# Two narrow projections as columns of wider groups, gate weights on two strips of rows, and other due tiles for VectorE

## Chip, cores and metric

One core of a Trainium2 chip runs one transformer stack of two different blocks for a batch of one with 256 tokens and a model width of 1024, in float32. The metric is the device time of one launch in microseconds (us), as the median of several runs.

## What is computed

The first block has attention over compressed, selected and window keys, retention, gates and an MLP. The change touches mainly the second block's mixer, in which one projection of the normed rows is split into ten parts:

```python
proj = n @ w_in
z, xBC, dt_raw, q, k, v, r, a1, g_ssd, g_gla = jnp.split(proj, idx, axis=-1)
# widths: z 1024, xBC 1536, dt_raw 16, q 512, k 512, v 1024, r 1024, a1 16, g_ssd 1024, g_gla 1024
# ssd: xBC = silu(causal conv of xBC);  dt = softplus(dt_raw + dt_bias);  a = -dt * exp(A_log)
#      y = (chunked scan of xs, B, C with steps dt and decays a) * silu(z), then a norm
# gla: log_alpha = log_sigmoid(a1 @ w_a2 + b_a) / 16;  w_a2 is 16 x 512
#      o = gated linear attention of q, k, v with these decays, normed, * silu(r)
merged = sigmoid(g_ssd) * (y_ssd @ w_up_ssd) + sigmoid(g_gla) * (y_gla @ w_up_gla)
```

In the kernel "the steps" are dt_raw (columns 2560 to 2575 of the weights) and "the gate's columns" are a1 (5648 to 5663).

## The kernel before

**Weights.** All 309 weight tiles go through one pipe, in one order. `weight` (L333) makes a tile of at most 1024 columns of float32 per partition. SyncE loads tile i into one of RAW = 4 raw buffers once VectorE has done tile i - 4 (L2318 is its issue). ScalarE rounds it to a high part (`round_tile`, L1014, instruction L1020), VectorE subtracts to get the low part (`rest_of_tile`, L1520, instruction L1524); both parts lie in one of PARTS = 5 buffers, which tile i gets when TensorE has released tile i - 5. A product is three matmuls: high by high, high by low, low by high.

**Groups.** `fm` (L353, matmuls L367 to L369) gives outputs with features on partitions: a group is 256 columns of weights, two tiles, 48 matmuls of 256 columns of tokens; the first tile is released after 36 of them, the second with the last. `tm` (L378, matmuls L398 to L400) gives outputs with tokens on partitions: a group of up to 512 columns of weights in two PSUM banks (one per half of the tokens), eight rows of blocks in four tiles, 12 matmuls a tile. `narrow` (L411) takes both sets of 16 columns as two tiles of 128 columns and 24 matmuls (L424 to L426).

**Order on TensorE.** `fill` (L792) is a chain of groups: z, gq, gk, gv, r, sig2, then a projection up. `step(n)` (L431) takes n steps from it, a step being a tile of tm or half a group of fm. The conv groups cv 2 to 5 are taken between by `conv()` (L788); cv 0 and 1 come ahead in `lead` (L479 to L481). From L796 on: a step, cv 2, two transposes that spread the rows' scales (L463), `narrow`, two steps, two transposes of the steps to tokens (L804), cv 3, two steps, cv 4, two steps, cv 5, two steps, then xs, the decays, and the loop over eight diagonal blocks (`diags`) with a step or two between and y's blocks turned by `y_out`. Behind it comes `la`, the product of wa2 (16 rows on partitions 0 to 15) with a1T, eight steps, the scores ST and ST2 of the gated attention (L350 is `group`, the helper of all small products) and its outputs.

**Order on ScalarE and VectorE.** Each goes through a list of operations written out in program order. Between them stand weight tiles: `until(v)` (L1023, L1527) first does all tiles whose parts buffer is released before TensorE's count v, and the drains "put behind" that are due before v, the earlier first and drains first at a tie; `full(name)` does `until` of that group's end and then waits for it. TensorE counts one for a released tile and one for an ended group.

```python
def until(v):
    while True:
        tile_at = gives_back(hi) if hi < len(tiles) else NEVER
        if min(tile_at, behind_at) >= v:
            return
        if behind_at <= tile_at:
            behind_at = next(behind, NEVER)
        else:
            round_tile()
```

ScalarE's list after the spread (L1314 on): conv copies of cv 0 and 1 (`conv_in`, L1306, two instructions each), two scaled copies of x (L1322), conv copies of cv 2, Exp of A_log (L1325), exponential of the steps (L1328), conv copies of cv 3, two silus (L1300), cv 4, and so on. Put behind: the drains of z with Silu (L1165), gv, r. VectorE's list: the spread copy (L1617), drains of conv groups into `craw` (L1558, a helper of all its two-operand instructions), for each group a conv of six L1564 (which waits for ScalarE's conv copies), the a1T drain (L1893), bias and minimum of the steps (L1898), a memset and the rest of the softplus. POOL computes a polynomial of it. Later VectorE adds up y's blocks, scales them (L1561), makes the operands ke and qe of the gated attention (L2067 on), and copies ST2 (L2078).

**In the first block** VectorE does `scores(1)`, `weigh(0)` and then for each p `weigh(p + 1)`, `scores(p + 2)`, with the due tiles only inside `scores` (L1779 on); ScalarE has an `until` of its own ahead of each exponential (L1227). L639 is the first matmul of the products with the values, which needs a copy of ScalarE (L1054).

## Time and profile before

| | us |
|---|---|
| three runs | 974.34, 974.57, 972.91 |
| median | 974.34 |
| the profiled execution | 972.9 |
| its span, first to last instruction | 971.1 |

The profile is one execution. A row of a timeline has the start in us from the span's start, the duration in us, the engine, the line, the operation, what it writes and reads, its shape and count, and in brackets idle time of the engine ahead of it with what ended that. PE is TensorE (PEld its weight loads), DVE VectorE, ACT ScalarE. Ends of matmuls are modelled and overlap, so the pace of matmuls is read from their starts. The granted clock of TensorE was 0.999 of full speed over the span.

### The profile page before, as it was taken

What the parts mean: (1) busy time and instruction counts of PE and PEld (TensorE: products, weight loads), DVE (VectorE), ACT (ScalarE), POOL (GpSimd) and SP (SyncE); (2) the same over time, 40 slices, a digit from 0 to 9 for tenths busy, and PEclk for the clock granted to TensorE, in tenths of its full rate; (3) what the DMA queues carried; (4) which work ended last, traced back from release to release, by engine and by line L of the source; (5) the groups of instructions that cost most, each with busy time, mean ns of one, the idle gap of its engine ahead of it and who ended that gap; (6) DMA issues with size and microseconds to landing.
All of it is one profiled execution on the core that took longest, in us unless ns stands there. A gap on an engine that the chain in (4) does not pass through costs nothing.

```text
span 971.1 us, 15946 instructions
## 1 busy us (share of the span) xinstructions
PE 959.3 (99%) x6548; PEld 869.1 (89%) x6548; DVE 626.0 (64%) x811; ACT 516.7 (53%) x785; POOL 59.8 (6%) x110
## 2 busy tenths in 40 slices
PE   9999999999999999999999999999999999999997
PEld 7877789989998888999988999998998899999996
DVE  5776775677555555778857787776554466555544
ACT  6576645656444544566865565644455445444443
POOL 3000001001000000304000002100000010000001
PEclk9999999999999999999999999999999999999999
DMA  9972635455665656466564455555655446565661
GB/s 307 311 237 65 181 108 163 164 174 176 212 191 181 188 181 189 124 196 190 155 194 132 129 173 187 159 184 172 200 164 157 125 153 215 177 198 172 194 194 44
DMA packets 135528, 170.37 MB, mean 175 GB/s; under 512 B 7856, under 2 KB 99296, under 8 KB 135456
## 3 DMA queue, kind: packets, MB, share of 16 engines
q1 hardware_dynamic: 133488, 165.20, 55.2%
q10 hardware_dynamic: 1424, 2.84, 0.8%
q0 software_dynamic: 544, 1.31, 0.4%
q8 instruction: 52, 0.85, 0.3%
q14 instruction: 20, 0.16, 0.1%
HBM read 168.28 MB, written 1.05 MB: 174 GB/s over the span
## 4 chain that ended last, share of the span: by engine, by line
PE 88%; DVE 5%; ACT 3%; issue 2%; POOL 0%; DMA 0%; ACTq 0%; POOLq 0%; DVEq 0%
PE ps L367 13%; PE ps L369 13%; PE ps L368 13%; PE ps L398 8%; PE ps L400 7%; PE ps L399 7%; PE ps L725 5%; PE ps L724 5%; PE ps L723 5%; PE ps L350 4%; PE ps L448 3%; DVE parts L1524 2%; DVE room L1558 2%; PE ps L479 1%; PE ps L481 1%
## 5 line engine op out<-in xcount | busy, mean ns | idle before, releaser
L1524 DVE TENSOR_TENSOR parts<-raws,parts 128x1024 fp32r<-128x1024 f32 (+2 forms) x309 | 367.8, 1207 | 233.0 <-ACT parts L1020 232.2
L1020 ACT ACTIVATE parts<-raws 128x1024 fp32r<-128x1024 f32 (+2 forms) x309 | 316.1, 1040 | 242.6 <-PE ps L369 136.2
L367 PE MATMUL ps<-room_r,parts 128*128 128x256 f32 x1248 | 352.2, 282 | 0.1
L368 PE MATMUL ps<-room_r,parts 128*128 128x256 f32 x1248 | 348.5, 279 | 0.0
L369 PE MATMUL ps<-room_r,parts 128*128 128x256 f32 x1248 | 348.4, 279 | 0.0
L367 PEld LDWEIGHTS ps<-room_r,parts 128*128 128x128 f32 x1248 | 234.6, 188 | 5.7 <-issue 3.9
L368 PEld LDWEIGHTS ps<-room_r,parts 128*128 128x128 f32 x1248 | 234.7, 188 | 1.3
L369 PEld LDWEIGHTS ps<-room_r,parts 128*128 128x128 f32 x1248 | 234.6, 188 | 0.0
L398 PE MATMUL ps<-parts,room_r 128*128 128x512 f32 (+1 forms) x336 | 134.8, 401 | 1.4 <-DVE parts L1524 1.4
L400 PE MATMUL ps<-parts,room_r 128*128 128x512 f32 (+1 forms) x336 | 131.1, 390 | 0.0
L399 PE MATMUL ps<-parts,room_r 128*128 128x512 f32 (+1 forms) x336 | 131.0, 390 | 0.0
L723 PE MATMUL ps<-parts,room_r 128*128 128x512 f32 x204 | 80.7, 396 | 0.0
L725 PE MATMUL ps<-parts,room_r 128*128 128x512 f32 x204 | 80.7, 396 | 0.0
L724 PE MATMUL ps<-parts,room_r 128*128 128x512 f32 x204 | 80.7, 396 | 0.0
L398 PEld LDWEIGHTS ps<-parts,room_r 128*128 128x128 f32 x336 | 63.2, 188 | 16.3 <-DVE parts L1524 2.4
L400 PEld LDWEIGHTS ps<-parts,room_r 128*128 128x128 f32 x336 | 63.1, 188 | 14.4
L399 PEld LDWEIGHTS ps<-parts,room_r 128*128 128x128 f32 x336 | 63.2, 188 | 13.2 <-issue 0.5
L1558 DVE TENSOR_TENSOR room_r<-room,room_r 128x512 fp32r<-128x512 f32 x43 | 29.8, 693 | 33.1 <-ACT room_r L1285 11.9
L725 PEld LDWEIGHTS ps<-parts,room_r 128*128 128x128 f32 x204 | 38.3, 188 | 9.3
L723 PEld LDWEIGHTS ps<-parts,room_r 128*128 128x128 f32 x204 | 38.3, 188 | 8.2
L724 PEld LDWEIGHTS ps<-parts,room_r 128*128 128x128 f32 x204 | 38.3, 188 | 8.1
L350 PE MATMUL ps<-room 128*128 128x256 f32 (+6 forms) x276 | 43.1, 311 | 0.7 <-DVE room L2078 0.7
(225 smaller groups left out, 877.5 us busy)
## 6 DMA issues: line engine op xcount, KB each, us to landing
raws<-in_w_in SPq DMA_DIRECT2D x99, 512.0 KB, 4.5
raws<-in_w_ffn_in SPq DMA_DIRECT2D x44, 512.0 KB, 4.4
raws<-in_w_up SPq DMA_DIRECT2D x32, 512.0 KB, 4.1
raws<-in_w_down SPq DMA_DIRECT2D x32, 512.0 KB, 4.1
raws<-in_w_ffn_out SPq DMA_DIRECT2D x22, 512.0 KB, 4.2
raws<-in_w_xkv SPq DMA_DIRECT2D x16, 512.0 KB, 4.1
raws<-in_w_out SPq DMA_DIRECT2D x8, 512.0 KB, 4.0
raws<-in_w_up_ssd SPq DMA_DIRECT2D x8, 512.0 KB, 4.5
```

The costliest lines, as they stand in the source:

```text
L350: last = e.matmul(ps, l, r, start=i == 0, stop=i == len(pairs) - 1)
L367: e.matmul(ps, wh, hT[0][:, k, :], start=k == 0, stop=False)
L368: e.matmul(ps, wh, hT[1][:, k, :], start=False, stop=False)
L369: last = e.matmul(ps, wl, hT[0][:, k, :], start=False, stop=k == K - 1)
L398: e.matmul(ps, hT[0][:, k, tok], wh, start=k == 0, stop=False)
L399: e.matmul(ps, hT[0][:, k, tok], wl, start=False, stop=False)
L400: last = e.matmul(ps, hT[1][:, k, tok], wh, start=False, stop=k == K - 1)
L723: e.matmul(ps, uh[:, k, tok], wh, start=q == 0 and k == 0, stop=False)
L724: e.matmul(ps, uh[:, k, tok], wl, start=False, stop=False)
L725: last = e.matmul(ps, ul[:, k, tok], wh, start=False, stop=q == n - 1 and k == 1)
L1020: e.activation(t.h, t.raw, ACT.Copy).then_inc(s["hi"], 1)
L1524: e.tensor_tensor(t.l, t.raw, t.h.bitcast(F32), ALU.subtract).then_inc(s["lo"], 1)
```

## The change

- The 16 columns of the steps become the last columns of z's first group, those of the gate the last of r's first group. z and r are now three groups each (THIRDS: 336, 352, 336 columns of their own, so 352, 352 and 336 with the added ones): 12 tiles and 144 matmuls each instead of 8 and 96. A tile of a first group is loaded by two DMAs.
- `narrow`, its two transposes and both its drains go.
- ScalarE drains the added columns: the steps straight into `dt3` (tokens on partitions already), the gate's columns of both halves of the tokens into `twice`. TensorE turns the latter to `a1T` in the loop at i = 7, VectorE copies that at i = 6 of its own list.
- The steps of `fill` are dealt out anew: 2, 2, 3, 3, 3 around the conv groups; two a round from i = 5 on; 4 after the loop.
- wa2 lies on two strips of rows (0 to 15 and 32 to 47), loaded by two DMAs; `la` goes strip by strip in turn.
- VectorE does due tiles after `weigh(0)`, with the bound that ScalarE has there, and ahead of ke and qe with ScalarE's bound instead of ST's end.

```diff
 
+        THIRDS = [(0, 336), (336, 352), (688, 336)]
...
+                elif also is not None:
+                    srcs = [(raw[:, :, 0:n - 16], src.rearrange("(k p) n -> p k n", p=P)),
+                            (raw[:, :, n - 16:n], also.rearrange("(k p) n -> p k n", p=P))]
...
-                for b0 in range(512 * first, cn, 512):
-                    nb = min(512, cn - b0)
+                spans = spans or [(b0, min(512, cn - b0)) for b0 in range(512 * first, cn, 512)]
+                for blk, (b0, n) in enumerate(spans, first):
+                    more = blk == 0 and also is not None
+                    nb = n + 16 if more else n
                     own = [bank(), bank()]
-                    tile_at = lambda k0, deep: weight(w[k0 * P:(k0 + deep) * P, c0 + b0:c0 + b0 + nb], deep, nb)
+
+                    def tile_at(k0, deep):
+                        rows_ = slice(k0 * P, (k0 + deep) * P)
+                        return weight(w[rows_, c0 + b0:c0 + b0 + n], deep, nb, also=w[rows_, also:also + 16] if more else None)
...
-            def narrow(name, parts_of, hT, ready):
...
-            fill = chain(tm("z", w2, 0, 1024, xT, x_ready(MIX2)), fm("gq", w2, 2576, 512, xT, x_ready(MIX2)),
+            fill = chain(tm("z", w2, 0, 1024, xT, x_ready(MIX2), spans=THIRDS, also=2560), fm("gq", w2, 2576, 512, xT, x_ready(MIX2)),
                          fm("gk", w2, 3088, 512, xT, x_ready(MIX2)), tm("gv", w2, 3600, 1024, xT, x_ready(MIX2)),
-                         tm("r", w2, 4624, 1024, xT, x_ready(MIX2)), fm("sig2", w2, 5664, 2048, xT, x_ready(MIX2)),
+                         tm("r", w2, 4624, 1024, xT, x_ready(MIX2), spans=THIRDS, also=5648), fm("sig2", w2, 5664, 2048, xT, x_ready(MIX2)),
                          fm(("first", 1), a["w_up_ssd_2"][0], 0, D, yT, lambda k: need(s["yT"], 4)))
-            step()
+            step(2)
             conv()
             spread_rstd(4, MIX2)
-            narrow("a1dt", [(w2, 5648), (w2, 2560)], xT, x_ready(MIX2))
-            step(2)
-            b = bank()
-            out_of("a1dt")
-            for t in range(2):
-                last = e.transpose(psum[:, b, 16 * t:16 * t + 16], a1T[32:48, t * P:t * P + P], ident[32:48, 32:48])
-            ends(last, "dt", b)
-            conv()
             step(2)
             conv()
-            step(2)
+            step(3)
             conv()
-            step(2)
+            step(3)
+            conv()
+            step(3)
...
-                step()
+                step(2 if i > 4 else 1)
                 if i == 7:
                     y_out(0, 1)
+                    need(s["a1"], 2)
+                    turn("a1T", [twice[:, half_, 0:48] for half_ in range(2)])
                 diag(t, q)
                 if i < 6:
                     step()
                 if i in (2, 4):
                     y_out(i // 2 - 1, 0)
-            step(3)
+            step(4)
             y_out(1, 1)
             step()
-            need(s["wa2"], 16)
-            for i in range(2):
-                b = bank()
-                for c in range(2):
-                    h = 2 * i + c
-                    last = group(psum[:, b, 256 * c:256 * c + 256], [(wa2[:, h * P:h * P + P], a1T[0:16, :])])
-                ends(last, ("la", i), b)
+            need(s["wa2"], 32)
+            out_of("a1T")
+            own = [bank() for _ in range(2)]
+            for c in range(2):
+                for i in range(2):
+                    h, strip = 2 * i + c, slice(32 * i, 32 * i + 16)
+                    last = group(psum[:, own[i], 256 * c:256 * c + 256], [(wa2[strip, h * P:h * P + P], a1T[strip, :])])
+                    if c:
+                        ends(last, ("la", i), own[i])
...
+            def thirds_out(dst, name, f, more, more_to):
+
+                for blk, (c0, n) in enumerate(THIRDS):
+                    for t in range(2):
+                        g = where[name, blk, t]
+                        yield g.at
+                        e.wait_ge(s["pe"], g.at)
+                        if blk == 0:
+                            to = more_to(t)
+                            e.activation(to, bc(psum[:, g.bank, n:n + 16], 1, list(to.shape)), ACT.Copy,
+                                         scale=scaled(MIX2, t)).then_inc(s[more], 1)
+                        e.activation(dst[:, t, c0:c0 + n], psum[:, g.bank, 0:n], f, scale=scaled(MIX2, t)).then_inc(taken[g.bank], 1)
+
             def projections2():
-                yield from tm_out(zs, "z", 2, MIX2, ACT.Silu)
+                yield from thirds_out(zs, "z", ACT.Silu, "dt", lambda t: dt3[:, t, :].unsqueeze(1))
                 yield from tm_out(gv, "gv", 2, MIX2)
-                yield from tm_out(gr, "r", 2, MIX2)
+                yield from thirds_out(gr, "r", ACT.Copy, "a1", lambda t: chunks(twice[:, t, 0:64], 2)[:, :, 0:16])
...
-            until(where["a1dt"].at + 1)
+            until(where["spread", MIX2].at + 2)
...
-            full("dt")
+            until(where["z", 0, 1].at + 1)
...
-            until(max(where["r", 1, 1].at + 1, where["la", 1].at + 6))
-            out_of(("r", 1, 1))
+            until(max(where["r", 2, 1].at + 1, where["la", 1].at + 6))
...
             scores(1)
             weigh(0)
+            until(where["S", 1, 1].at + 3)
...
-            full("a1dt")
-            emptied(tt(a1T[0:48, :], bank_of("a1dt")[0:48, 0:256], rows_rstd[0:48, :], ALU.mult), "a1dt")
             conv(0)
             conv_in(2)
-            until(where["a1dt"].at + 1)
+            until(where["spread", MIX2].at + 2)
             conv(1)
-            full("dt")
-            emptied(tt(dt3, bank_of("dt")[:, 0:32].rearrange("p (t h) -> p t h", t=2),
-                       bc(row("ssd_dt_bias_2"), 1, [P, 2, 16]), ALU.add), "dt")
-            out_of("dt")
+            until(where["z", 0, 1].at + 1)
+            e.wait_ge(s["dt"], 2)
+            step(tt(dt3, dt3, bc(row("ssd_dt_bias_2"), 1, [P, 2, 16]), ALU.add))
+            settle()
             stt(e_, dt_, -1.0, dt_, ALU.mult, ALU.min).then_inc(s["soft_e"], 1)
...
-                out_of(("z", 0, t))
-                out_of(("z", 1, t))
+                for blk in range(3):
+                    out_of(("z", blk, t))
...
+                if i == 6:
+                    full("a1T")
+                    emptied(e.tensor_copy(a1T[0:48, :], bank_of("a1T")[0:48, 0:256]), "a1T")
...
-            until(where["ST", 0].at)
+            until(max(where["r", 2, 1].at + 1, where["la", 1].at + 6))
...
```

The rest of the diff names the semaphore "a1", makes wa2 48 rows high and loads its two halves on POOL's queue.

## Rows read from the trace of the kernel before

**Rows 1.** The page's first part: each engine's busy us, and granted clock by slice

```profile
PE 959.3 (99%) x6548; PEld 869.1 (89%) x6548; DVE 626.0 (64%) x811; ACT 516.7 (53%) x785; POOL 59.8 (6%) x110
...
PEclk9999999999999999999999999999999999999999
```

**Rows 2.** Waits of TensorE: waited for, us in total, times, longest us

```profile
PE ps L639 <- ACT room L1054: 2.2, 1, 2.2
...
PE ps L398 <- DVE parts L1524: 1.4, 2, 0.8
...
PE ps L350 <- DVE room L2078: 0.7, 1, 0.7
```

**Rows 3.** Timelines of VectorE, ScalarE and TensorE, 92 to 100 us

```profile
92.22 0.18 DVE L1809 RECIPROCAL room<-room 128x4 f32<-128x4 f32 x1 [3.74 <-ACT big L1227]
...
93.25 4.62 DVE L1524 TENSOR_TENSOR parts<-raws,parts 128x1024 fp32r<-128x1024 f32 x4
...
98.14 1.06 ACT L1020 ACTIVATE parts<-raws 128x1024 fp32r<-128x1024 f32 x1 [5.07 <-DMA raws<-in_w_in]
...
99.73 0.49 PE L639 MATMUL ps<-room 120*128 120x128 f32 x2 [2.15 <-ACT room L1054]
```

**Rows 4.** Timeline of TensorE, 410 to 428 us, around the narrow product

```profile
410.63 0.39 PE L398 MATMUL ps<-parts,room_r 128*128 128x512 f32 x1
...
413.43 0.28 PE L367 MATMUL ps<-room_r,parts 128*128 128x256 f32 x1
...
419.17 0.36 PE L424 MATMUL ps<-room_r,parts 128*48 128x256 f32 x1
...
422.04 0.40 PE L398 MATMUL ps<-parts,room_r 128*128 128x512 f32 x1
...
427.74 0.29 PE L804 MATMUL ps<-ident,room 16*128 16x16 f32 x2
```

**Rows 5.** Timeline of ScalarE, 422 to 443 us

```profile
422.79 2.08 ACT L1306 ACTIVATE room<-room,cols 128x256 f32<-128x256 f32 x4 [2.44 <-DVE room L1558]
...
426.67 2.18 ACT L1322 ACTIVATE x<-room,ssq 128x1024 f32<-128x1024 f32 x2
...
429.85 1.28 ACT L1325 ACT_TABLE_LOAD   x1
...
441.30 1.28 ACT L1165 ACT_TABLE_LOAD   x1
...
442.60 1.26 ACT L1165 ACTIVATE room<-ps,ssq 128x512 f32<-128x512 f32 x2
```

**Rows 6.** Timeline of VectorE, 438 to 444 us

```profile
438.46 0.69 DVE L1558 TENSOR_TENSOR room<-ps,rows_rstd 128x512 f32<-128x512 f32 x1
...
443.05 1.22 DVE L1524 TENSOR_TENSOR parts<-raws,parts 128x1024 fp32r<-128x1024 f32 x1
```

**Rows 7.** Groups by line and shape: us busy, mean ns, idle before

```profile
L1020 ACT ACTIVATE parts<-raws 128x1024 fp32r<-128x1024 f32 x301 | 311.5, 1052 | 236.1 <-PE ps L369 136.2 <-PE ps L400 33.6 <-PE ps L725 33.4
...
L1524 DVE TENSOR_TENSOR parts<-raws,parts 128x1024 fp32r<-128x1024 f32 x301 | 363.1, 1223 | 232.0 <-ACT parts L1020 231.3
```

**Rows 8.** Timeline of TensorE: the gate product, and the first block's scores

```profile
545.70 1.99 PE L350 MATMUL ps<-room,wa 16*128 16x256 f32 x8
...
85.06 0.70 PE L613 MATMUL ps<-room 64*128 64x256 f32 x4
```

**Rows 9.** Timeline of VectorE, 572 to 577 us

```profile
572.87 2.36 DVE L1524 TENSOR_TENSOR parts<-raws,parts 128x1024 fp32r<-128x1024 f32 x2 [4.24 <-ACT parts L1020]
...
576.88 0.42 DVE L1558 TENSOR_TENSOR room<-room 128x256 f32<-128x256 f32 x1
```

**Rows 10.** Timelines of VectorE and TensorE around y's fourth turn

```profile
540.91 0.49 DVE L1561 TENSOR_SCALAR room<-room,ssq 128x512 f32<-128x512 f32 x1 [1.78 <-POOL ssq L2186]
...
542.36 0.60 PE L448 MATMUL ps<-ident,room 128*128 128x128 f32 x4
```

32 lines of the change are left out of this document (10 added, 22 removed).

## The prediction

> **What bounds the kernel now.** The page's first part is read first: TensorE is busy for 959.3 of 971.1 us, and its granted clock is at 9 tenths or more in all 40 slices [rows 1]. So TensorE's own columns set the time, and an edit counts where it takes instructions from that queue or makes it stand still. The waits of TensorE are read second: over 0.5 us there are few [rows 2]. L639 stands 2.2 us for a copy of ScalarE, L398 0.8 us (the longer of two) for VectorE's rest of a weight tile, L350 0.7 us for VectorE's last copy before the outputs of the gated attention. Third, the timelines of the other two engines around these places. Each works through a list in the program's order, and a weight tile needs both: ScalarE rounds it, VectorE takes the rest, and only then do its raw buffer (one of four) and, after its matmuls, its parts buffer (one of five) come free. What one engine does ahead of a tile is harmless only while TensorE has tiles in hand.
>
> **Part 1, due tiles before the first softmax (gain).** VectorE stands idle 3.74 us until 92.22, then weighs and takes four tiles in a row from 93.25 to 97.87, three of which ScalarE had rounded before its scores. ScalarE's next tile then waits 5.07 us for its DMA (98.14), whose raw buffer had been held by the first of the four, and TensorE's pv product stands until 99.73 behind it [rows 3]. The new `until` lets VectorE take the three in the idle time: 88.5 to 91.9, done before 92.22. The raw buffer is free at 89.6 instead of 94.4, and as release to rounding was 98.14 - 94.4 = 3.7 us, ScalarE has the tile at 93.3 and the copy by 94.9. TensorE starts its next tile without the 0.8 of L398 [rows 2], at 93.7, ends it at 96.5 and finds the copy there: 99.73 - 96.55 = 3.2, I take 3.1 us. Late next is nothing: VectorE's scores and ScalarE's exponentials move up by as much. Ends: 2.2 (the longer wait alone) and 3.3.
>
> **Part 2, columns.** Twelve matmuls of 512 columns take 410.63 to 413.43, so 0.2333 us each, 0.456 ns a column; the 48 of 256 behind them and two small transposes take until 419.17, 0.117 us each [rows 4]: time goes by columns, and nothing is charged per instruction at either width. So 352 columns are 0.160 us, 336 are 0.153. z was 96 x 512 columns, now 48 x 1040: 768 more, +0.35 us; r the same, +0.35. The narrow product goes: 419.17 to 422.04, -2.87 us, and its two transposes with the gaps around them, -0.4 [rows 4]. The new a1T turn adds two transposes of 0.11 each, +0.25 with its gap. Sum -2.3. Should 352 columns be charged like 512, z and r would cost 144 x 0.2333 instead of 96 x 0.2333, +11 each; the row of 256 excludes that.
>
> **Part 3, z's first group now holds the steps' columns (loss).** This is the large term, and I walk it in the clock of before; all of it hangs on order. TensorE, without waits: z0 and z1 (1.92 each) 410.63 to 414.5, conv group 2 (5.6) to 420.1, transposes to 420.2, z2 and z3 to 424.1, conv group 3 to 429.7, z4 and z5 to 433.55. Then it wants z6, whose parts buffer was z3's (free at 424.1).
> ScalarE [rows 5]: its four conv copies began at 422.79; one more tile ahead of VectorE's spread copy makes that 423.15. Copies 2.05, z5's tile 0.8, the two of L1322 2.1, conv copies 1.1, Exp's table load with its operation 1.4: 430.5. Now comes `until(where["z", 0, 1].at + 1)`, and the drains of z's first group are due before z6's tile: two copies of the steps 0.25, a load of Silu's table 1.28, two drains 1.05, so z6 is rounded from 433.0 to 433.8. Before, both drains came at 442.60, with the load of 441.30, after the exponential of the steps; now they stand between two Exp, so the exponential (L1328) and the first silu each need a load again: two more loads, 2.6 us. VectorE's rest: until 434.7. **Wait 1: 1.2 us.**
> VectorE adds the bias and makes its minimum (0.3), ScalarE waits for that, loads Exp (1.28), exponentiates (0.15) and only then rounds the next conv tile, 436.5 to 437.55; rest until 438.8. TensorE has wanted it since 434.8 + 1.92: **wait 2: 2.1 us.**
> VectorE drains group 3, from then on as before: from drain over ScalarE's copies and the conv to the tile behind it 443.05 - 438.46 = 4.6 us [rows 6]. The second tile of conv group 4 sits in the buffer of group 3's second tile, whose release is that group's very end, so both engines take it only after their conv work (before, it came a place sooner): 438.75 + 4.6 + 1.2 = 444.55 against a want at 438.9 + 1.4: **wait 3: 4.3 us.**
> The same pattern in group 5 leaves 0.5: its first tile's raw buffer is free at 444.55, landing and rounding take some 5.1, so its rest ends at 450.9; drain, conv and the tile behind (4.3 without the small work of group 3, and 1.2) give 456.4. TensorE ends group 4 at 448.8 and z7 to z9 at 454.5, and wants it at 455.9. **Wait 4: 0.5 us.** Sum +8.1 us. Tiles of 704 columns are taken as 0.80 on ScalarE and 0.89 on VectorE, from 1052 and 1223 ns for 1024 [rows 7]; 0.1 us either way moves each wait by as much. Bounds: 0 if the other order of drain and tile held, and 10.7 if either added load cost twice its row. The POOL queue gets one small DMA more and SP's queue eight pieces with 64-byte rows; they sit in transfers that land some us before their tile's turn.
>
> **Part 4, second gate weights.** Eight instructions on one strip take 545.70 to 547.62 [rows 8]. The scores of the first block use two strips: four take 0.70 us, the two first starting together. On strips the product of the gates should take about 1.05, -0.85 us; 0 if sixteen rows don't run side by side.
>
> **Part 5, later due tiles.** VectorE waits 4.24 us for ScalarE until 572.87 and makes the four decayed operands at 576.88, 1.1 us, after the tiles [rows 9]. With the smaller bound they go into the idle time, and the ST2 copy behind L350's wait [rows 2], which starts at 582.02, ends at 581.6 instead of 582.7. TensorE, earlier by part 4, then wants it at 582.0: the stall of 0.9 (the wait and its start) goes. Next late are tiles with about 1 us in hand.
>
> **Part 6, r and the turn.** From the turn of y's third block to that of the fourth TensorE has 9.3 us of work instead of 10.15 (four tiles of 336 columns for three of 512), and VectorE's chain there had y scaled at 541.4 against a turn at 542.36 [rows 10], with 0.4 added by the copy of a1T: +0.4 us. Ends 0 and 2.
>
> **Sum.** -3.1 - 2.3 + 8.1 - 0.85 - 0.9 + 0.4 = +1.35 us, taken as +1.4. The profiled execution was 972.9 us (span 971.1), hence 974.3; the median of the three runs is 974.34, 1.4 above it, so the forecast for a median is 975.7. About 0.2% (1.9 us) is what a measurement of this kernel can tell from no change, so this is no change.
>
> **A page that speaks against it.** After the load at 441.30 + 1.28 = 442.58 the drain starts at 442.60 [rows 5]: the load costs its own length. The Trainium skill's ScalarE: Activation LUTs, under What ACT_TABLE_LOAD costs, charges every switch of sets with 1283 ns and a drain of about 1380 more. By that rule the two new loads would cost 5.3 us instead of 2.6 and the result would be 978.4. As a mechanism of this kernel: an idle stretch of 1.4 us behind either load, passed on to waits 1 and 2. The rows speak against it, chance 0.02.
>
> **Rivals.** A, the forecast (0.55): own range 972.5 to 979. B, faster (0.23): ScalarE's delay is eaten by tiles in hand, or the conv tiles come in time; then the sum is 1.4 - 8.1 = -6.7, 967.6. For it: at present TensorE has no wait at all in this stretch, and the tiles in hand cover several us. Against: cover is five tiles, and z's have shrunk from 2.8 to 1.92 us each. C, slower (0.10): r's tiles are too short as well. Between conv and gate TensorE has 1.9 us per tile instead of 2.8 while ScalarE waits 3 to 4 us at a time on y's squares; once an engine is away from tiles for over 4 x 1.92 us plus the products between, TensorE stops. Two such stops of 1.5 us give +3: 978.7. D (0.05): part 1 does not do what it says, because the DMA and not VectorE's order was the limit; +3.1: 978.8. Against: that DMA began only after VectorE's release. E (0.05): TensorE's clock, at its upper level (2.4 GHz) in all slices now, even across the stand before 99.73, falls to the lower (1.2) during wait 3, twice as long; at half speed each us of matmuls costs another, and some 3 us of that give 978.7. The Trainium skill's TensorE: Matmul & The Clock Gate, under The HAM clock gate, has an idle array clocked down; no row here shows it in mid-kernel.
> Faster by over 0.2%: B and 0.06 of A, 0.29. Slower: C, D, E, the page's rule and 0.18 of A, 0.40. Within: 0.31. The range of 967 to 980 takes in B's centre, the slower rivals and the bounds of A.
>
> **What would show it.** Right: TensorE's waits at 94 to 100 gone, z and r at 0.16 us a matmul, four loads of tables between 425 and 450, and VectorE's rest of a tile as releaser of waits of some 1, 2 and 4 us between 430 and 445. Wrong: no wait over 1 us there (B), waits in the tiles of r (C), L639 still waiting (D), or 352 columns at over 0.17 us.

## The result: slower by half a per cent, and the profile after

The changed kernel took 978.59 us (median of 977.9, 979.1, 979.22 and 978.08) against 974.04 for the kernel before beside it: ratio 1.0048, 95% interval 1.0031 to 1.0065. So it is slower, by 4.5 us, where the forecast was 975.7 and no change; the range of 967 to 980 holds it. The profiled execution took 977.9 us with a span of 976.1, 5.0 more than before.

The page's first part and TensorE's granted clock by slice, as in [rows 1]:

```profile
PE 958.8 (98%) x6620; PEld 876.2 (90%) x6620; DVE 626.5 (64%) x817; ACT 522.1 (53%) x801; POOL 58.0 (6%) x111
...
PEclk9999999999999999999999999999999999999999
```

TensorE is as busy as before though it has fewer columns to go through. The waits of TensorE, to hold against [rows 2] (waited for, us in total, times, longest):

```profile
PE ps L373 <- DVE parts L1529: 6.7, 4, 4.0
PE ps L412 <- DVE parts L1529: 2.1, 2, 1.1
...
PE ps L442 <- DVE room L1566: 0.4, 1, 0.4
```

L639's wait (now L633) is gone, and VectorE's rest of a tile stands behind nearly all that is new: 8.8 us, of which 1.1 lies at the very start of the kernel (at 7.70; the kernel before waits 0.6 there). Where the rest is, the timeline of TensorE shows. A stand, a stretch in which TensorE starts nothing, is read here from start to start, less one matmul's own pace (437.14 to 441.40 is 4.26, less 0.12: 4.15 us); the idle time in brackets is 0.15 less, since it counts from a modelled end.

```profile
96.76 0.39 PE L633 MATMUL ps<-room 120*128 120x128 f32 x2
...
407.56 0.32 PE L412 MATMUL ps<-parts,room_r 128*128 128x352 f32 x1
407.72 0.33 PE L413 MATMUL ps<-parts,room_r 128*128 128x352 f32 x1
...
431.84 0.43 PE L412 MATMUL ps<-parts,room_r 128*128 128x352 f32 x1 [1.01 <-DVE parts L1529]
...
435.78 0.36 PE L373 MATMUL ps<-room_r,parts 128*128 128x256 f32 x1 [1.72 <-DVE parts L1529]
...
437.14 0.28 PE L375 MATMUL ps<-room_r,parts 128*128 128x256 f32 x1
441.40 0.58 PE L373 MATMUL ps<-room_r,parts 128*128 128x256 f32 x1 [3.99 <-DVE parts L1529]
...
442.00 0.41 PE L375 MATMUL ps<-room_r,parts 128*128 128x256 f32 x1
...
444.55 0.28 PE L375 MATMUL ps<-room_r,parts 128*128 128x256 f32 x1
...
546.86 0.66 PE L442 MATMUL ps<-ident,room 128*128 128x128 f32 x4 [0.43 <-DVE room L1566]
...
550.25 1.13 PE L356 MATMUL ps<-room,wa 16*128 16x256 f32 x8
...
571.79 0.36 PE L373 MATMUL ps<-room_r,parts 128*128 128x256 f32 x1 [0.43 <-DVE parts L1529]
...
573.97 0.39 PE L373 MATMUL ps<-room_r,parts 128*128 128x256 f32 x1 [0.54 <-DVE parts L1529]
```

The first product with the values starts 3.0 us sooner than in [rows 3]. A matmul of 352 columns takes 0.16 us. Then come the stands: 1.2 us before 431.84, 1.9 before 435.78, 4.15 before 441.40, 0.6 at y's fourth turn (546.86), 0.6 and 0.7 before two tiles of the gates (571.79, 573.97). And behind the longest one matmuls of 256 columns follow each other at 0.213 us (442.00 to 444.55 are twelve of them) instead of 0.117. The windows say why (length, busy us of PE, PEld, DVE, ACT and POOL, granted clock, DMA share, GB/s):

```profile
442.00:444.00 2.00, 2.00 (x11) 2.00 (x11) 1.90 (x7) 0.82 (x2) 0.05 (x1) 0.50 0.68 187
...
446.00:450.00 4.00, 4.00 (x30) 4.00 (x30) 1.87 (x2) 2.00 (x3) 3.23 (x10) 1.00 0.57 172
```

For 3.4 us, from about 441 on, TensorE ran at its lower clock level (1.2 GHz). The page's slices of 24 us each still print a 9: a fall this short is seen only in windows.

ScalarE in the same stretch, to hold against [rows 5]:

```profile
427.48 0.26 ACT L1310 ACTIVATE room<-ps,ssq 128x16 f32<-128x16 f32 x1
427.75 1.28 ACT L1312 ACT_TABLE_LOAD   x1
429.05 0.54 ACT L1312 ACTIVATE room<-ps,ssq 128x336 f32<-128x336 f32 x1
...
430.88 1.28 ACT L1333 ACT_TABLE_LOAD   x1
432.18 0.23 ACT L1333 ACTIVATE room<-room 128x32 f32<-128x32 f32 x1
432.31 1.04 ACT L1012 ACTIVATE parts<-raws 128x1024 fp32r<-128x1024 f32 x1
...
437.33 2.37 ACT L1012 ACTIVATE parts<-raws 128x1024 fp32r<-128x1024 f32 x3
```

Two loads (427.75, 430.88) stand between the copies of the steps and the exponential, as the forecast had it, and the next operation starts 1.30 us after the start of each. And VectorE, against [rows 6] and, for the last two rows, [rows 10] and [rows 9]:

```profile
432.04 2.46 DVE L1569 SCALAR_TENSOR_TENSOR room<-room,cols 128x256 f32<-128x256 f32 x6
434.41 1.22 DVE L1529 TENSOR_TENSOR parts<-raws,parts 128x1024 fp32r<-128x1024 f32 x1
...
437.45 2.46 DVE L1569 SCALAR_TENSOR_TENSOR room<-room,cols 128x256 f32<-128x256 f32 x6 [1.22 <-ACT room L1298]
...
440.14 2.78 DVE L1529 TENSOR_TENSOR parts<-raws,parts 128x1024 fp32r<-128x1024 f32 x3
...
546.72 4.62 DVE L1529 TENSOR_TENSOR parts<-raws,parts 128x1024 fp32r<-128x1024 f32 x4
...
570.43 1.21 DVE L1529 TENSOR_TENSOR parts<-raws,parts 128x1024 fp32r<-128x1024 f32 x1
```

The tile that ends wait 3 is the first of the three at 440.14. ScalarE had rounded it by 438.3; VectorE took it only after the convolution of group 3 (437.45). The tile that ends wait 2 was rounded at 432.31, done by 433.4, and taken by VectorE at 434.41, after the convolution of group 2 (432.04).

The four tiles at 546.72 stand between VectorE's scaling of y and the next operation of y's chain. In the kernel before they are three, behind the scaling at 540.91 [rows 10]:

```profile
541.31 2.35 DVE L1524 TENSOR_TENSOR parts<-raws,parts 128x1024 fp32r<-128x1024 f32 x2
544.23 1.23 DVE L1524 TENSOR_TENSOR parts<-raws,parts 128x1024 fp32r<-128x1024 f32 x1 [0.57 <-ACT parts L1020]
```

### The profile page after: what moved, and what is told of

Its sections match the earlier page's. It is cut to its first block, busy times and chain, and to the rows that moved or that the text cites. A ratio compares the mean times of both kernels' runs of the same rounds, so it can differ in the third digit from the quotient of the medians.

```text
span 976.1 us, 16142 instructions
## 1 busy us (share of the span) xinstructions
PE 958.8 (98%) x6620; PEld 876.2 (90%) x6620; DVE 626.5 (64%) x817; ACT 522.1 (53%) x801; POOL 58.0 (6%) x111
## 4 chain that ended last, share of the span: by engine, by line
PE 91%; DVE 4%; ACT 2%; issue 1%; DMA 1%; SPq 0%; POOL 0%; POOLq 0%; DVEq 0%; ACTq 0%
PE ps L373 14%; PE ps L374 14%; PE ps L375 14%; PE ps L412 7%; PE ps L413 7%; PE ps L414 7%; PE ps L718 5%; PE ps L719 5%; PE ps L717 5%; PE ps L356 5%; PE ps L442 3%; DVE parts L1529 1%; PE ps L473 1%; PE ps L475 1%; PE ps L474 1%; DVE room L1563 1%
## 5 line engine op out<-in xcount | busy, mean ns | idle before, releaser
L1529 DVE TENSOR_TENSOR parts<-raws,parts 128x1024 fp32r<-128x1024 f32 (+4 forms) x315 | 368.4, 1187 | 239.1 <-ACT parts L1012 237.8
L1012 ACT ACTIVATE parts<-raws 128x1024 fp32r<-128x1024 f32 (+4 forms) x315 | 317.1, 1024 | 243.7 <-PE ps L375 137.9
L412 PE MATMUL ps<-parts,room_r 128*128 128x512 f32 (+3 forms) x368 | 140.7, 382 | 2.4 <-DVE parts L1529 2.1
L414 PE MATMUL ps<-parts,room_r 128*128 128x512 f32 (+3 forms) x368 | 136.6, 371 | 0.0
L413 PE MATMUL ps<-parts,room_r 128*128 128x512 f32 (+3 forms) x368 | 136.5, 371 | 0.0
L412 PEld LDWEIGHTS ps<-parts,room_r 128*128 128x128 f32 x368 | 69.2, 188 | 15.4 <-DVE parts L1529 3.6
L414 PEld LDWEIGHTS ps<-parts,room_r 128*128 128x128 f32 x368 | 69.1, 188 | 11.5
L413 PEld LDWEIGHTS ps<-parts,room_r 128*128 128x128 f32 x368 | 69.2, 188 | 10.7 <-issue 0.5
L719 PEld LDWEIGHTS ps<-parts,room_r 128*128 128x128 f32 x204 | 38.3, 188 | 9.3
L718 PEld LDWEIGHTS ps<-parts,room_r 128*128 128x128 f32 x204 | 38.3, 188 | 8.2
L717 PEld LDWEIGHTS ps<-parts,room_r 128*128 128x128 f32 x204 | 38.3, 188 | 8.2
```

The source lines that it names most:

```text
L412: e.matmul(ps, hT[0][:, k, tok], wh, start=k == 0, stop=False)
L413: e.matmul(ps, hT[0][:, k, tok], wl, start=False, stop=False)
L414: last = e.matmul(ps, hT[1][:, k, tok], wh, start=False, stop=k == K - 1)
L717: e.matmul(ps, uh[:, k, tok], wh, start=q == 0 and k == 0, stop=False)
L718: e.matmul(ps, uh[:, k, tok], wl, start=False, stop=False)
L719: last = e.matmul(ps, ul[:, k, tok], wh, start=False, stop=q == n - 1 and k == 1)
```

## Experiments

Each time is a median and stands beside runs of the kernel before on the same chip. The chips are not the same throughout, so it is the ratio to the kernel before that is compared from one experiment to another; the changed kernel's is 1.0048. "Less than the change" is the difference of the ratios in us. Rows are from one profiled execution of each kernel.

### The two bounds alone

The kernel before, with

```diff
             weigh(0)
+            until(where["S", 1, 1].at + 3)
...
-            until(where["ST", 0].at)
+            until(max(where["r", 1, 1].at + 1, where["la", 1].at + 6))
```

> The kernel before with the change's two VectorE bounds and nothing else. My theory: the first (three due tiles before the first softmax) gives 3.1 to 3.2 us at the first product with the values, the second (due tiles ahead of the four decayed operands) some 0.9 us at the ST2 copy; together about -4, 970 against a before of 974. Rival (the DMA of the tile was the limit, and the 3.2 us came from elsewhere in the change): no difference at the first product, about 973 to 974. Rival on the second bound: with the gate product on one strip nothing is gained there, -3.1.

Measured: 968.74 us against 973.84, ratio 0.9944 (0.9932 to 0.9956), the fastest kernel of this study. VectorE:

```profile
88.50 3.49 DVE L1524 TENSOR_TENSOR parts<-raws,parts 128x1024 fp32r<-128x1024 f32 x3
92.33 0.18 DVE L1809 RECIPROCAL room<-room 128x4 f32<-128x4 f32 x1 [0.34 <-ACT big L1227]
...
577.73 0.68 DVE L2079 COPY room<-ps 128x512 f32<-128x512 f32 x1
```

The three tiles now lie in what was idle time, and the reciprocal waits 0.34 us instead of 3.74 [rows 3]. TensorE's first product with the values starts at 96.61, 3.12 us sooner, and later landmarks 3.22 sooner, until the last bound adds its 0.9 at the outputs: the copy of ST2 ends at 578.41, and TensorE starts the outputs without a stand at 578.83. The span is 4.4 us shorter; the medians differ by 5.1, of which 0.7 is the spread between executions. Parts 1 and 5 are as predicted, each to 0.1 us, and the rival on the DMA is out. So all that belongs to the columns and to the strips costs 9.4 us of span (976.1 - 966.7).

### Silu drains of z later

```diff
-                yield from thirds_out(zs, "z", ACT.Silu, "dt", lambda t: dt3[:, t, :].unsqueeze(1))
+                for t in range(2):
+                    g = where["z", 0, t]
+                    yield g.at
+                    e.wait_ge(s["pe"], g.at)
+                    e.activation(dt3[:, t, :], psum[:, g.bank, 336:352], ACT.Copy, scale=scaled(MIX2, t)).then_inc(s["dt"], 1)
+                for blk, (c0, n) in enumerate(THIRDS):
+                    for t in range(2):
+                        g = where["z", blk, t]
+                        yield max(g.at, where["cv", 3].at + 1)
...
```

> The changed kernel, with ScalarE's six Silu drains of z held back until the first tile of conv group 3 is released; only the two copies of the steps are made when z's first group ends. No load of a table stands between the spread and the softplus any more. Theory (each of the three waits is set by what the two engines do ahead of one certain tile): wait 1 (1.17 us at z's seventh tile) goes, wait 2 (1.9) shrinks to about 1.2, wait 3 (4.15, at the second tile of conv group 4) stays, and so does the stretch at the lower clock: -1.7 us, about 976.9 against 978.6. Rival (the table loads and drains are the root of all three waits): all go, -7 or more, about 971.

Measured: 975.7 us, ratio 1.0019 (1.001 to 1.0028), 2.8 us less than the change. Stands: wait 1 gone, wait 2 at 0.9, wait 3 still 4.15, and again 3.4 us at the lower clock behind it. So the added loads and drains make wait 1 and half of wait 2, and nothing of wait 3. The rival is out. By the trace it gained 2.35 us in this stretch where I had 1.7: wait 2 shrank by 1.0 and not 0.7, and my two terms, 1.2 and 0.7, already made 1.9.

### The tile ahead of the convolution of group 3

```diff
# ScalarE
+            until(where["cv", 3].at + 1)
             conv_in(3)
# VectorE
             conv_in(3)
+            until(where["cv", 3].at + 1)
             conv(3)
```

> The changed kernel, with one more bound on ScalarE (ahead of its copies of conv group 3) and one on VectorE (ahead of the convolution of group 3): the tile whose buffer comes free with the first half of conv group 3 is done before that convolution and not after it. Theory: wait 3 falls from 4.15 us to 0.3 to 1, TensorE's clock does not fall behind it (3.4 us at the lower level, worth about 1.5), waits 1 and 2 stay: -4.5 to -5.3, 973.3 to 974.1. Rival (the tile is late by its landing or by what both engines did before, not by the place of the convolution): within 1 us of 978.6. Rival (the clock falls for the sum of the three waits, not for the third): 3.4 to 4 us gained and the stretch at the lower clock still there.

Measured: 973.68 us, ratio 0.9997 (0.9988 to 1.0006), 5.0 less than the change: one tile moved past one convolution takes back the whole loss, within the intervals. VectorE, and TensorE behind it:

```profile
436.96 1.21 DVE L1530 TENSOR_TENSOR parts<-raws,parts 128x1024 fp32r<-128x1024 f32 x1
438.27 2.46 DVE L1570 SCALAR_TENSOR_TENSOR room<-room,cols 128x256 f32<-128x256 f32 x6
```

```profile
450.99 0.39 PE L373 MATMUL ps<-room_r,parts 128*128 128x256 f32 x1 [1.26 <-DVE parts L1530]
```

This execution is 0.8 us behind the changed kernel's at wait 1 already (432.66 to 431.84); so the tile, done at 438.17, is ready some 4 us sooner than there (441.3). The clock stays at its upper level, waits 1 and 2 are as they were (1.2 and 1.9). From z's first matmul to the turn of xs the trace has 3.9 us less, the medians more; 4 to 5 us is what can be said. The price shows at 450.99: 1.4 us at the second tile of conv group 5, which is the forecast's wait 4. In the changed kernel it was hidden, since wait 3 and the slow matmuls gave the two engines over 5 us there.

### z without its silu

```diff
-                yield from thirds_out(zs, "z", ACT.Silu, "dt", lambda t: dt3[:, t, :].unsqueeze(1))
+                yield from thirds_out(zs, "z", ACT.Copy, "dt", lambda t: dt3[:, t, :].unsqueeze(1))
```

> The changed kernel with z drained by a plain scaled copy: it leaves out the silu of z, and with it both added table loads (2.6 us of ScalarE). The drains stay where they are. Theory: ScalarE has z's seventh tile 1.3 us earlier, wait 1 (1.17) goes, but what each engine does ahead of the conv tiles is as before, so waits 2 and 3 stay within 0.5 us: -1.2, about 977.4. Rival (the two loads are the whole loss, 2.6 us on ScalarE's path that all three waits repeat): waits 2 and 3 go too, 971 or less.

Measured: 977.06 us, ratio 1.0034 (1.0022 to 1.0046), 1.4 less than the change. Wait 1 is gone, wait 2 is 1.7, wait 3 4.15 with 3.4 us at the lower clock. ScalarE has 2.6 us less work, and 1.3 us come of it in this stretch: its load alone is not the point.

### The gate product on one strip

```diff
-                    h, strip = 2 * i + c, slice(32 * i, 32 * i + 16)
+                    h, strip = 2 * i + c, slice(0, 16)
```

> The changed kernel with both halves of the gate product on one strip of rows again (rows 0 to 15). Theory: TensorE takes 1.92 us for the eight instead of 1.06, but the two waits behind it (0.59 and 0.70 us) shrink by nearly as much, since both engines' work is what they hang on: within 0.3 us of the changed kernel's 978.6. Rival (the strips' gain is real on the path): 979.4.

Measured: 978.43 us, ratio 1.004 (1.0027 to 1.0053), within the intervals the same as the change. TensorE:

```profile
550.94 1.99 PE L356 MATMUL ps<-room,wa 16*128 16x256 f32 x8
...
574.66 0.38 PE L373 MATMUL ps<-room_r,parts 128*128 128x256 f32 x1 [0.34 <-DVE parts L1529]
```

The eight take 1.92 us again, but the stand before the first of the two tiles of the gates is gone and the second is 0.5 us instead of 0.7. The stand before the outputs is 0.4 us, as on two strips. From the start of the gate product to the first ST group the two kernels need 25.32 and 25.33 us: the 0.86 us of the strips are real on TensorE and worth nothing on the path. (In this execution the lower clock held for 6.8 us around the end of wait 3, from 439.5 on, at the same stands; its span is 0.9 us longer than the changed kernel's.)

### All three waits mended in the changed order

The late Silu drains, here from `where["cv", 3].at + 3` on, and:

```diff
# ScalarE
-            until(where["z", 0, 1].at + 1)
+            until(where["cv", 3].at + 1)
             e.wait_ge(s["soft_e"], 1)
             e.activation(e_, e_, ACT.Exp).then_inc(s["soft_exp"], 1)
-            conv_in(3)
             until(where["cv", 3].at + 3)
+            conv_in(3)
# VectorE
+            until(where["cv", 3].at + 1)
             conv(2)
             conv_in(3)
+            until(where["cv", 3].at + 3)
             conv(3)
```

> The changed kernel with all orders of this stretch mended: Silu drains of z later, the exponential of the steps and the convolutions of groups 2 and 3 behind the tiles that are due by the first and third count of conv group 3. Theory: waits 1 to 3 and the lower clock go, 7.2 + 1.5 us; what is left are the three waits of 0.6 to 0.7 us late in the diagonal blocks: about 970.0 against 978.6, and below the kernel before (974.0) by 4. Rival (the lateness only moves on, to conv groups 4 and 5 or the diagonal blocks, since both engines have the same work to do): 973 to 976.

Measured: 972.95 us, ratio 0.9989 (0.998 to 0.9998); one of the eleven runs took 4273.5 us, no trace shows why, and it doesn't move the median. Waits 1 to 3 are gone, and a new one of 2.7 us stands before conv group 5's second tile, with 3.4 us at the lower clock behind it:

```profile
446.26 4.02 DVE L1539 TENSOR_TENSOR parts<-raws,parts 128x1024 fp32r<-128x1024 f32 x4
```

```profile
447.59 0.39 PE L373 MATMUL ps<-room_r,parts 128*128 128x256 f32 x1 [2.56 <-DVE parts L1539]
```

The rival was right: the lateness moved on by one group. The four tiles at 446.26 come behind the convolution of group 4, just as wait 3's tile came behind that of group 3.

### Another deal of the steps

```diff
             conv()
-            step(3)
+            step(2)
             conv()
-            step(3)
+            step(2)
             conv()
-            step(3)
+            step(5)
```

> The changed kernel with the steps around the conv groups dealt 2, 2, 2, 2, 5 instead of 2, 2, 3, 3, 3, and nothing else; same tiles, same work, another order. Theory: with three steps between, the second tile of conv group 4 takes the parts buffer that the very end of group 3 gives back, five tiles earlier; with two steps it takes that of group 3's first tile, given back a quarter of a group earlier, and TensorE has 9.4 us of work between the end of group 3 and the next tile that hangs on it. So wait 3 (4.15 us) and the stretch at the lower clock (1.5) go, wait 2 (1.9) is under 0.5, wait 1 stays at 1.2 to 1.5: -6.8 to -7.3, about 971.5 against 978.6. Rival (each engine is short of time over the whole stretch, and the deal only chooses where it shows): waits of 3 us and more remain elsewhere between 430 and 460, 974 to 977.

Measured: 976.35 us, ratio 1.002 (1.0011 to 1.0029), 2.7 less than the change and not 7 (the spans of the two traces differ by 1.4). VectorE and TensorE:

```profile
432.70 2.46 DVE L1569 SCALAR_TENSOR_TENSOR room<-room,cols 128x256 f32<-128x256 f32 x6
435.08 1.22 DVE L1529 TENSOR_TENSOR parts<-raws,parts 128x1024 fp32r<-128x1024 f32 x1
```

```profile
432.61 0.36 PE L373 MATMUL ps<-room_r,parts 128*128 128x256 f32 x1 [1.72 <-DVE parts L1529]
...
436.36 0.39 PE L373 MATMUL ps<-room_r,parts 128*128 128x256 f32 x1 [2.11 <-DVE parts L1529]
```

The stands are 1.9, 2.3 and, before gq's first tile at 460.5, 1.5, and the clock fell for 3.4 us behind the second. Here I had miscounted: TensorE wants the second tile of a conv group 1.4 us after the first (12 matmuls), not 4.2. So wait 2 did not shrink but grew; it is the tile at 435.08, behind the convolution of group 2. The tile that made wait 3 makes none here, as the buffer rule says.

### The deal with late Silu drains, and a bound that moved nothing

The first run joins the deal with the late drains (from `where["cv", 3].at + 3` on); the second adds, on ScalarE ahead of the wait for y_sum and on VectorE ahead of that for y_rstd:

```diff
+                if n == 3:
+                    until(where["yx", 1].at + 1)
```

> As the run with the deal 2, 2, 2, 2, 5, and ScalarE's Silu drains of z held back until two tiles behind conv group 3, so that there is no pair of added table loads. Theory: wait 1 goes too, 1.2 to 1.5 us less than with the deal alone: about 970.2. Rival: the drains now stand in a heap behind group 3 (six in a row, 3.2 us) and make a tile late there, no gain over the deal alone or a loss of up to 1.

> As the run with the deal and the late Silu drains, and in the last diagonal block both engines do one due tile ahead of their wait in the chain of y's norm (ScalarE idle 3.9 us there, VectorE 1.8). Theory: VectorE has three tiles instead of four between its scaling of y and the gain of y's fourth turn, so the additions of the gate product start 1.2 us earlier and the waits of 0.6 and 0.7 us at two tiles of the gates' groups go: 1.0 to 1.3 less than without, about 969. Rival: those two waits hang on the later chain of exponentials and scans, not on its start: no change.

Measured: 974.45 and 974.28 us, both ratio 1.0004 (0.9995 to 1.0012, and 0.9994 to 1.0013). The late drains gave 1.9 us (these three kernels ran on one chip), and the stand before gq's first tile is hardly longer (1.7 us, 1.5 with the deal alone), so they made no heap that costs. The second run told nothing of its question: `until` takes only tiles released before its count, none was under this one, and all engines had the same instructions in the same order as in the first. But as a repeat it shows something. Both executions have the same stand of 1.94 us before the second tile of conv group 4, and differ in this, here for 434 to 436 us in the first and in the second:

```profile
434.00:436.00 2.00, 2.00 (x11) 2.00 (x12) 0.78 (x2) 1.43 (x3) 0.00 (x0) 0.57 0.43 78
```

```profile
434.00:436.00 2.00, 1.33 (x11) 1.33 (x12) 1.21 (x2) 0.69 (x2) 0.00 (x0) 1.00 0.20 17
```

In the first the clock was at the lower level for 3.4 us behind that stand, in the second not at all.

### Three moves, and then the tile ahead of group 3 as well

On top of the deal and the late drains:

```diff
# ScalarE, ahead of the exponential; VectorE, ahead of the bias
-            until(where["z", 0, 1].at + 1)
+            until(where["cv", 3].at)
# ScalarE
-            for q in range(3, 6):
-                silu(q)
+            silu(3)
+            silu(4)
+            until(where["cv", 5].at + 1)
+            silu(5)
# VectorE
+            until(max(where["r", 2, 1].at + 1, where["la", 1].at + 6))
             e.wait_ge(s["khexp"], 1)
             tt(kh, kh, gk, ALU.mult).then_inc(s["kh"], 1)
-            until(max(where["r", 2, 1].at + 1, where["la", 1].at + 6))
```

> The run with the deal 2, 2, 2, 2, 5 and the late Silu drains (waits left there: 1.94 us at the second tile of conv group 4 with 3.4 us at the lower clock behind it, 1.69 at gq's first tile, 0.59 and 0.70 at two tiles of the gates), with three moves: both engines do the tile that is due before conv group 3 ends ahead of the softplus' minimum and exponential; ScalarE does the tile due behind conv group 5 ahead of its last silu; VectorE does one due tile ahead of its product of kh with k. Theory: the first takes away the wait of 1.94 and the clock's fall (1.5), the second 1.7, the third 0.7: about -5.5, 968.9, as fast as the kernel before with the two bounds alone (968.7). Rival (every place mended makes the next one late, because the lateness is in both engines' load): -2, 972 to 973.

Measured: 973.47 us, ratio 0.9995 (0.9987 to 1.0004). The three stands went, and another came, 3.1 us at z's next tile, with the clock at the lower level for 6.8 us. That is near the rival's 972 to 973, and not the forecast's 968.9:

```profile
435.37 2.46 DVE L1581 SCALAR_TENSOR_TENSOR room<-room,cols 128x256 f32<-128x256 f32 x6 [1.23 <-ACT room L1298]
...
438.06 2.82 DVE L1541 TENSOR_TENSOR parts<-raws,parts 128x704 fp32r<-128x704 f32 x3
```

```profile
438.99 0.66 PE L412 MATMUL ps<-parts,room_r 128*128 128x352 f32 x1 [2.98 <-DVE parts L1541]
```

It is once more a tile behind the convolution of group 3 (438.06, free since that group's end). The third move took away the stand of 0.7 and made that before the outputs 1.0 instead of 0.4. Hence the next run, with the two bounds of the run on wait 3 added and the third move taken back:

> The run with the three moves, in which TensorE waited 3.14 us at z's next tile behind conv group 4 (ScalarE had rounded it, VectorE took it only after the convolution of group 3), and in which the clock was at the lower level for 6.5 us behind that. Added: the two bounds that the run on wait 3 had, the tile released by the end of conv group 3 is done by ScalarE ahead of its copies of that group and by VectorE between its drain and the convolution. Taken back: the move ahead of kh, which only moved its 0.6 us to the outputs. Theory: the wait and the clock's fall go, 3.1 + 3.2 us, and 0.1 comes back: about 967.2, 7 below the kernel before (974.4) and 1.5 below the kernel before with the two bounds alone. Rival (it moves on once more, to conv group 4 or 5): 970 to 973.

Measured: 971.91 us, ratio 0.9978 (0.9969 to 0.9987). It beats the kernel before, and not the two bounds alone; it is in the rival's range, 4.7 us above the forecast of 967.2. The clock does not fall in the profiled execution, and what is left is small but in many places:

```profile
439.15 0.43 PE L412 MATMUL ps<-parts,room_r 128*128 128x352 f32 x1 [1.01 <-DVE parts L1542]
...
447.94 0.40 PE L412 MATMUL ps<-parts,room_r 128*128 128x336 f32 x1 [0.74 <-DVE parts L1542]
```

1.2 and 0.9 us here, 0.4 at 455.83, 0.6 at y's turn, 0.5 and 0.7 at the gates, 0.4 at the outputs: 4.7 us, where the kernel with the two bounds alone has no wait over 0.4. With some 2 us less work on TensorE the span is 3.1 us longer.

### Tiles really moved in the last block

On top of that run, with counts that tiles fall under (3 on ScalarE, 2 on VectorE):

```diff
# ScalarE, ahead of the wait for y_sum
+                if n == 3:
+                    until(where["yx", 1].at + 3)
# VectorE, ahead of the wait for y_rstd
+                if n == 3:
+                    until(where["yx", 1].at + 2)
```

> The last run had 971.9 us, with waits of 0.55 and 0.70 us at two tiles of the gates. The earlier try to move tiles into the idle times of the last diagonal block had a bound that no tile fell under: the order of instructions was that of the run without it, so it was a repeat and told nothing of this question. Here the bounds are two and one counts higher: ScalarE does two tiles ahead of its squares of y's last block (idle 3.9 us), VectorE one ahead of the scaling (idle 1.8). Theory: three tiles instead of four lie between VectorE's scaling and the gain of y's fourth turn, the additions of the gate product start 1.2 us earlier relative to TensorE, and both waits at the gates' tiles go: -1.0 to -1.3, about 970.8. Rival (they hang on the order further down, ahead of kh): no change, 971.9. Second rival: the tile makes y's scaling late, y's fourth turn waits 0.6 us longer and takes half of the gain.

Measured: 970.85 us, ratio 0.9961 (0.9948 to 0.9975). VectorE and TensorE:

```profile
539.24 1.22 DVE L1544 TENSOR_TENSOR parts<-raws,parts 128x1024 fp32r<-128x1024 f32 x1
541.17 0.49 DVE L1581 TENSOR_SCALAR room<-room,ssq 128x512 f32<-128x512 f32 x1 [0.72 <-POOL ssq L2211]
541.58 3.49 DVE L1544 TENSOR_TENSOR parts<-raws,parts 128x1024 fp32r<-128x1024 f32 x3
```

```profile
541.72 0.66 PE L442 MATMUL ps<-ident,room 128*128 128x128 f32 x4 [0.50 <-DVE room L1581]
```

One tile went ahead of the scaling (539.24) and three are left behind it instead of four. The two stands at the gates' tiles are gone but for 0.2 us, y's fourth turn waits 0.07 us longer, and from the gate product to the first ST group TensorE needs 24.19 us instead of 25.32: 1.1 us, as the first theory had it. The times agree (971.91 before it, 970.85 now), but the intervals of the two ratios overlap, so it is the trace that shows it.

## Why the prediction was near, and where it was short

The span grew by 5.0 us and the sum was +1.4. Term by term:

| step of the prediction | forecast | measured |
|---|---|---|
| part 1 | -3.1 | -3.2 |
| part 2, columns | -2.3 | about -1.6 |
| part 3, waits 1 to 4 | 1.2, 2.1, 4.3, 0.5 | 1.2, 1.9, 4.15, 0 |
| rival E, clock (not in the sum) | +3 | +1.5, it happened |
| part 4, strips | -0.85 | -0.86 on TensorE |
| part 5 | -0.9 | -0.5 |
| part 6 | +0.4 | +0.6 |
| two tiles of the gates | not seen | +1.3 |
| start and loads of inputs | none | +0.25, and 0.2 before the last MLP |

**Right.** The rows of before carried the large terms. Wait 3 was derived from one pair of rows [rows 6] and a buffer rule of the kernel, and it came within 0.15 us; the run with the tile ahead of the convolution shows that this order is its cause (the wait gone, 5.0 us back). That the added drains and loads make wait 1 is shown by the run with late drains. The doubt about the table loads is settled: the load at 427.75 ends at 429.03 and its drain starts at 429.05, that at 430.88 is followed at 432.18. By the Trainium skill's ScalarE: Activation LUTs, under What ACT_TABLE_LOAD costs, there would be some 1380 ns more behind each; this trace has none of it.

**Right by luck: wait 2.** The number is near (2.1 against 1.9), the working is not. The forecast had ScalarE wait for VectorE's minimum and only then load Exp's table, which put its rounding of the tile 1.1 us too late. In the trace the load (430.88) runs beside VectorE's work, and the tile is rounded at 432.31. But the forecast let VectorE take the rest at once, and it took it 1.1 us later, after the convolution of group 2, as for wait 3. The two errors cancel. It is also why the late drains took only half of wait 2 away.

**The step that failed: the clock was left out of the sum.** Rival E had 0.05, because the clock had stood through the stand before 99.73. It should have been a part of forecast A, since A itself held a stand of 4.3 us. Its price was also off. The forecast had each us of matmuls cost another, for 3 us of matmuls; the fall lasted 3.4 us, of which 0.3 lay in the stand, and in the rest half the work was done: 1.5 us lost. With that the sum is +2.9. The reason for the 0.05 rested on one execution, and the runs of the kernel before fall into two kinds: of the 17 beside the run without silu, eight had spans of 970.9 to 971.6 us at a mean granted clock of 0.999, and nine had 972.6 to 974.0 at 0.996 to 0.998. The profiled one is of the first kind. With the two bounds alone, which remove the stand, all five spans lie within 966.6 to 967.6. So in the second kind the clock probably did fall behind that stand, and the 1.4 us that the forecast added between its profiled execution and the median was probably the price of it. No execution of that kind was traced, so this is not shown.

**The second: part 4 was put on the path.** The forecast took 0.85 us off and asked only what part 5 would then do. It did not ask who has to keep up with a TensorE that is 0.86 us ahead. The chain of the second mixer does not run on TensorE: VectorE takes the tiles at 546.72 between scaling y and the gain of its fourth turn, so it starts the additions of the gate product no earlier, and its tiles come late at 571.79 and 573.97, +1.3 us for the two stands. The run on one strip shows it: 0.86 us put back, and TensorE is at the first ST group at the same distance. The strips are not all of it, for on one strip 0.5 us of stand stays. That fits the fourth tile: from VectorE's scaling to the gain are 4.94 us, before 4.46. The last run points to the same place: with one of the four tiles ahead of the scaling the stands go and 1.1 us come back. So the strips' gain can be had, but only with an order that lets VectorE keep up. The 0.4 us that stayed of part 5's 0.9 are another matter: that stand is there on one strip too, and in the last run, and why VectorE's copy of ST2 is late there is not shown.

**The third: part 2.** The pace is as predicted (0.160 and 0.153 us), but not every matmul keeps it. From start to start and without the stands, z's 144 matmuls take 23.15 us (its 96 before: 22.4) and r's 23.65 (before: 23.1), so both together cost 1.3 us more and not 0.7, which is nearly all that the part is short of. The first matmuls of some tiles take about 0.1 us more than the pace (417.20 to 417.45 is 0.25), which I had costed at nothing; whether that is all of it is not shown.

**Wrong, but small: wait 4.** It was in the sum at 0.5 and did not come; without wait 3 it is 1.4 us. The forecast did not carry on what its own wait 3 does, which is to give the other engines time.

**The rivals.** B had 0.23 for tiles in hand eating the delay: they ate none of waits 1 to 3. C's mechanism (r's tiles too short) is absent, TensorE has no stand over 0.6 us among r's tiles. D is out by the run of the two bounds. The chance of 0.40 for slower was fair, but 0.17 of it stood on C, D and the rule on table loads, which did not come, and 0.05 on E, which did. That the range of 967 to 980 holds the result owes as much to its width as to the sum.

## What to carry to other kernels

When two engines pass tiles to a third from lists written out by hand, a cut of the third one's work can turn into waits unless the lists are ordered anew: most places mended here sent a wait one group on (0.9997, 0.9989, 1.0020, 0.9995), and only many of them together came clearly below the kernel before (0.9978, 0.9961). Ask for each late tile what its engine does first, not how loaded the engine is: one tile moved past one convolution gave 4 to 5 us, 2.6 us less work on ScalarE gave 1.4 (and for wait 2 the tile was late on VectorE, not on ScalarE). And test the parts of a change by themselves: two bounds on VectorE were worth 5.1 us (0.9944), the rest of the change cost it all and more, and in the best order tried it still did not pay (0.9961, though the two intervals just overlap).

## What was not expected of the hardware

Whether TensorE's clock falls behind a stand is not decided by the length of the stand alone. Stands between 430 and 462 us, and time at the lower level, of the profiled executions:

| kernel | stands, us | lower level, us |
|---|---|---|
| changed | 1.2, 1.9, 4.15 | 3.4 |
| one strip | 1.2, 1.9, 4.15 | 6.8 |
| silu late | 0.9, 4.15 | 3.4 |
| no silu | 1.7, 4.15 | 3.4 |
| tile ahead of conv 3 | 1.2, 1.9, 1.4 | none |
| all waits | 2.7 | 3.4 |
| deal | 1.9, 2.3, 1.5 | 3.4 |
| deal, silu late | 1.9, 1.7 | 3.4 |
| the same order again | 1.9, 1.1, 2.1 | none |
| three moves | 3.1 | 6.8 |
| all moves | 1.2, 0.9, 0.4 | none |
| and tiles really moved | 1.2, 0.9, 0.5 | none |

In these executions all stands of 2.3 us and more have a fall with them, and of those of 1.9 one has, while the same order of instructions had none in another execution. The stand of the kernel before ahead of 99.73 is 2.3 us too by this measure (97.18 to 99.73, less 0.23), and the clock stayed up through it. A mean clock of 1.000 and one of 0.995 stand side by side among the runs of the three moves (spans 970.7 and 972.8), so that a fall comes each time is not shown even for 3.1 us. Where the clock fell, the stand cost some 1.5 us more than itself, and about twice that in two executions, and this may be what sets executions of one kernel apart, as with the two kinds of the kernel before above: the changed kernel's four had spans of 976.1 and 976.3 us at a mean clock of 0.997 and 0.998, and of 977.3 and 977.4 at 0.996. The Trainium skill's TensorE: Matmul & The Clock Gate, under The HAM clock gate, has an idle array clocked down to 1.2 GHz; the runs agree, and show it in mid-kernel behind a single stand of 1.9 us (deal, silu late).
